# Root-mean-square norm moved behind the up projections of two feed-forward blocks

## The reference, cut to what matters

```
# first block (D_FF = 2816)
xn = rms_norm(h, g_ffn) * (1.0 + sc2) + sh2        # rms_norm: h * rsqrt(mean(h*h) + EPS) * g
up = causal_dwconv(jnp.dot(xn, w_up), conv_ffn_w, conv_ffn_b)      # 3 taps over positions
val, gte = jnp.split(up, 2, axis=-1)
h = h + ga2 * jnp.dot(jax.nn.silu(gte) * val, w_down)
# second block
u2 = rmsnorm(h, ffn_norm_w)
a, val = jnp.split(u2 @ w_up, 2, axis=-1)
a = causal_dwconv_2(a, ffn_conv_w, ffn_conv_b)
h = h + (jax.nn.silu(a) * val) @ w_down
```

## Time and profile before

| | |
|---|---|
| median of 3 runs | 1895.46 us (1890.78 to 1900.73) |
| profiled execution, its own time | 1897.88 us |
| its span, first to last instruction | 1896.1 us |
| TensorE (PE) busy | 1804.7 us, 95% |
| GpSimd (POOL) busy | 1412.7 us, 75% |
| VectorE (DVE) busy | 942.8 us, 50% |
| ScalarE (ACT) busy | 641.6 us, 34% |
| mean granted TensorE clock | 0.974 of 2.4 GHz |

### The profile page before, as it was taken

The page is one execution under the profiler, slowest core; times in us unless marked ns, Lnnn a source line. Parts: engine busy times, 40 slices in busy tenths (PEclk is TensorE's granted clock), DMA queues, the critical chain, the costliest instruction groups (busy, mean ns, idle before and its releaser), DMA issues.

```text
span 1896.1 us, 31183 instructions
## 1 busy us (share of the span) xinstructions
PE 1804.7 (95%) x10268; PEld 1541.9 (81%) x10268; DVE 942.8 (50%) x1508; ACT 641.6 (34%) x870; POOL 1412.7 (75%) x2245
## 2 busy tenths in 40 slices
PE   4999998999889999999899999999999899999997
PEld 2767775578678888887899999999999889999885
DVE  6538887745554444311655654665654333333101
ACT  3236662310144444201533443344342233333100
POOL 2768982469968888899666775776776588888885
PEclk8999997999999999999999999999999899999999
DMA  8332332334422323233122222222222222323332
GB/s 319 110 107 94 95 106 100 100 133 155 155 74 92 94 94 100 90 109 100 56 68 78 78 67 67 68 78 68 75 71 68 67 89 88 100 88 94 103 102 88
DMA packets 54298, 184.40 MB, mean 97 GB/s; under 512 B 6673, under 2 KB 7857, under 8 KB 54226
## 3 DMA queue, kind: packets, MB, share of 16 engines
q1 hardware_dynamic: 48690, 169.20, 28.0%
q10 hardware_dynamic: 5536, 14.16, 2.1%
HBM read 178.62 MB, written 4.72 MB: 97 GB/s over the span
## 4 chain that ended last, share of the span: by engine, by line
PE 67%; POOL 14%; issue 10%; DMA 3%; DVEq 2%; DVE 2%; ACT 1%; SPq 1%; POOLq 0%; ACTq 0%
PE gp L373 21%; PE gp L374 21%; PE gp L375 20%; POOL Wlo L364 9%; POOL Whi L361 3%; PE A L673 3%; DMA raw<-units 2%; POOL probe L360 2%; DVEq L1415 2%; DMA AW<-ada 1%; PE A L702 0%; PE A L721 0%; SPq L309 0%; DVE XX L1413 0%; PE A L723 0%
## 5 line engine op out<-in xcount | busy, mean ns | idle before, releaser
L364 POOL TENSOR_TENSOR Wlo<-raw,Whi 128x256 fp32r<-128x256 f32 x1120 | 932.9, 854 | 46.7
L373 PE MATMUL gp<-XNhi,Whi 128*128 128x264 f32 (+3 forms) x2384 | 790.6, 332 | 44.9 <-DVE XNlo L1063 33.2
L374 PE MATMUL gp<-XNlo,Whi 128*128 128x264 f32 (+3 forms) x2384 | 781.0, 328 | 0.0
L375 PE MATMUL gp<-XNhi,Wlo 128*128 128x264 f32 (+3 forms) x2384 | 777.5, 326 | 0.0
L373 PEld LDWEIGHTS gp<-XNhi,Whi 128*128 128x128 f32 x2384 | 455.0, 191 | 96.1 <-issue 30.1
L374 PEld LDWEIGHTS gp<-XNlo,Whi 128*128 128x128 f32 x2384 | 455.2, 191 | 40.0 <-issue 1.9
L375 PEld LDWEIGHTS gp<-XNhi,Wlo 128*128 128x128 f32 x2384 | 454.4, 191 | 38.4
L360 POOL TENSOR_TENSOR probe<-raw 1x1 f32<-1x1 f32 x560 | 156.2, 279 | 415.5 <-PE gp L375 374.1
L361 POOL TENSOR_SCALAR Whi<-raw 128x512 fp32r<-128x512 f32 x560 | 347.0, 620 | 0.0
L374 PE MATMUL gp<-AClo,Whi 128*128 128x512 f32 x352 | 139.9, 397 | 0.0
L373 PE MATMUL gp<-AChi,Whi 128*128 128x512 f32 x352 | 139.9, 397 | 0.0
(11 more groups left out here) (291 smaller groups left out, 2261.4 us busy)
## 6 DMA issues: line engine op xcount, KB each, us to landing
raw<-units SPq DMA_DIRECT2D x280, 512.0 KB, 3.5
AW<-ada SPq DMA_DIRECT2D x16, 512.0 KB, 8.8
AWL<-ada SPq DMA_DIRECT2D x16, 512.0 KB, 4.0
AWL<-ada ACTq DMA_DIRECT2D x16, 512.0 KB, 4.3
bias_rows<-RB ACTq DMA_DIRECT2D x1, 2560.0 KB, 15.0
H<-xT SPq DMA_DIRECT2D x1, 2048.0 KB, 8.7
BIAS<-bias_rows ACTq DMA_DIRECT2D x1, 2048.0 KB, 9.6
out<-H SPq DMA_DIRECT2D x8, 256.0 KB, 2.1
```

The lines of the kernel that those rows point to most:

```text
L364: ins = pool.tensor_tensor(lo[:, c:c + UNIT // 4], src[:, c:c + UNIT // 4], hi[:, c:c + UNIT // 4].bitcast(F32), ALU.subtract)
L373: pe.matmul(dst, Whi[s][:, k, :], rhi, start=start, stop=False)
L374: pe.matmul(dst, Whi[s][:, k, :], rlo, start=False, stop=False)
L375: return pe.matmul(dst, Wlo[s][:, k, :], rhi, start=False, stop=stop)
```

## The change

For norms 1 and 3 (`WEIGHTED`), those of the two up projections, `norm_split` and `norm_apply` go. As soon as a chunk of H is final, during OUT1 and OUT2, ScalarE makes XNhi = H * factor behind the square, and VectorE XNlo = H * factor - XNhi behind the residual. TensorE does the statistics in the middle of the first pair of UP instead of ahead of it. For norms 2 and 4 nothing moves.

The outputs are multiplied by RSTD on VectorE on their way from PSUM to a buffer ZZ in SBUF, and all convolution taps then read ZZ instead of PSUM. In UP1 both units of a pair are 514 columns wide instead of 512: the two columns ahead of the first position (meta positions 14 and 15) hold the shift vector, so that the output there is W(s). BC = W(s) * (sum of the three taps, TAPS) + bias is the activation's bias, and ZZ's two first columns are -W(s), which cancels it where the convolution looks ahead of the first position. The meta columns of XN, written early before, are written after UP1. A PSUM buffer is freed by the product with RSTD. ScalarE's Silu table is loaded ahead of both loops. Semaphores, the two buffers' declarations and unchanged neighbours are left out here:

```diff
--- before.py
+++ after.py
+        TAPS = sb("TAPS", [P, FC, 2])
+        BC = sb("BC", [P, 2])
...
+            ZZ = sb("ZZ", [P, 2, 2 + S], frame=f)
...
+        WEIGHTED = (1, 3)
...
                 return mm
 
-            def first_pair(u0, g0, f, halves):
+            def first_pair(u0, g0, f, halves, midway=None):
 
                 lag = 1
                 for j in range(KC + lag):
+                    if j == KC // 2 and midway is not None:
+                        midway()
                     for c, k in ((0, j), (1, j - lag)):
                         if 0 <= k < KC:
...
-            def with_stats(m, product, begin):
+            def all_units(product, begin):
 
                 begin(product)
                 with pe.Fori(1, KC // 2) as i:
                     product(i, 0)
                     product(i, 1)
-                stats(m)
...
-            def up(u0, g0, f, halves):
-
-                first_pair(u0, g0, f, halves)
+            def up(u0, g0, f, halves, m):
+
+                first_pair(u0, g0, f, halves, lambda: stats(m))
                 with pe.Fori(1, FC) as i:
                     for c, (n, c0) in enumerate(halves):
                         pe.wait_ge(gp_free[c], slot_free(g0) + i)
                         unit(u0 + i * 2 + c, c, gp[c], n, XNhi, XNlo, c0, range(KC), last=KC - 1).then_inc(unit_done, 1)
 
-            with_stats(1, *plain(U_OUT, G_OUT, MGhi, MGlo, 0, S, (merge_done, 1)))
-            up(U_UP, G_UP, 1, ((S, META), (S, META)))
-            with_stats(2, *down(U_DN, G_DN, (act_done, 1)))
+            all_units(*plain(U_OUT, G_OUT, MGhi, MGlo, 0, S, (merge_done, 1)))
+            up(U_UP, G_UP, 1, ((S + 2, META - 2), (S + 2, META - 2)), 1)
+            all_units(*down(U_DN, G_DN, (act_done, 1)))
+            stats(2)
...
-            with_stats(3, *plain(U_OUT2, G_OUT2, M2hi, M2lo, META - 2, S + 2, (mix2_done, 1)))
-            up(U_UP2, G_UP2, 3, ((S + 2, META - 2), (S, META)))
-            with_stats(4, *down(U_DN2, G_DN2, (act2_done, 1)))
+            all_units(*plain(U_OUT2, G_OUT2, M2hi, M2lo, META - 2, S + 2, (mix2_done, 1)))
+            up(U_UP2, G_UP2, 3, ((S + 2, META - 2), (S, META)), 3)
+            all_units(*down(U_DN2, G_DN2, (act2_done, 1)))
+            stats(4)
...
                     h = H[:, k, q["c0"]:q["c0"] + q["n"]]
                     act.activation(sq[:, k % 2, 0:q["n"]], h, ACT.Square).then_inc(sq_ready, 1)
+                    if m in WEIGHTED:
+                        act.activation(XNhi[:, k, q["c0"]:q["c0"] + q["n"]], h, ACT.Identity,
+                                       scale=scale_bias(m, k)[0]).then_inc(xhi_ready, 1)
...
-                    act.wait_ge(nt_ready, KC * f + k + 1)
+                    act.wait_ge(nt_ready, KC * (f // 2) + k + 1)
                     act.activation(XNhi[:, k, o0:o0 + n], nt[:, k % 3, 0:n], ACT.Identity,
...
             norm_stats(1, lambda k: load_late(3 * KC + 2 + k) if k < KC - 2 else None)
-            norm_apply(1)
-
+
+            act.preload_act_table(ACT.Silu)
             with act.Fori(0, FC) as i:
-                def fv(c):
-                    return V[:, bass.ds(VEC["ffn"] + i * 8 + c, 1)]
-                act.wait_ge(unit_done, U_UP + i * 2 + 1 + 2)
-                act.wait_ge(act_done, i + 1)
-                act.activation(YV[:, :], gp[0][:, 0:S], ACT.Identity, bias=fv(3), scale=fv(2)).then_inc(yv_first, 1)
-                act.wait_ge(unit_done, U_UP + i * 2 + 2 + 2)
-                act.activation(YG[:, :], gp[1][:, 0:S], ACT.Identity, bias=fv(7), scale=fv(6)).then_inc(yg_first, 1)
+                for c, (y, first) in enumerate(((YV, yv_first), (YG, yg_first))):
+                    act.wait_ge(z_ready, i * 2 + c + 1)
+                    if c == 0:
+                        act.wait_ge(act_done, i + 1)
+                    act.activation(y[:, :], ZZ[:, c, 2:2 + S], ACT.Identity, bias=BC[:, c:c + 1],
+                                   scale=V[:, bass.ds(VEC["ffn"] + i * 8 + (4 * c + 2), 1)]).then_inc(first, 1)
                 act.wait_ge(yg_ready, i + 1)
                 act.activation(SL[:, :], YG[:, :], ACT.Silu).then_inc(silu_ready, 1)
             norm_stats(2)
@@ -1026,15 +1036,14 @@
                     act.activation(HRS[:, :], HRS[:, :], ACT.Exp, scale=-0.5).then_inc(orstd_ready, 1)
 
             norm_stats(3)
-            norm_apply(3)
-
+
+            act.preload_act_table(ACT.Silu)
             with act.Fori(0, FC) as i:
                 def fw(c):
                     return V[:, bass.ds(VEC["ffn2"] + i * 4 + c, 1)]
-                b0 = region(S + 2)
-                act.wait_ge(unit_done, U_UP2 + i * 2 + 1 + 2)
+                act.wait_ge(z2_ready, i + 1)
                 act.wait_ge(act2_done, i + 1)
-                act.activation(YV[:, :], gp[0][:, b0 + 2:b0 + 2 + S], ACT.Identity, bias=fw(3), scale=fw(2)).then_inc(ya_first, 1)
+                act.activation(YV[:, :], ZZ[:, 0, 2:2 + S], ACT.Identity, bias=fw(3), scale=fw(2)).then_inc(ya_first, 1)
                 act.wait_ge(ya_ready, i + 1)
                 act.activation(SL[:, :], YV[:, :], ACT.Silu).then_inc(silu2_ready, 1)
             norm_stats(4)
...
                         dve.scalar_tensor_tensor(hk, src, MOD[:, bass.ds(gate + i * 2 + c, 1)], hk, ALU.mult,
                                                  ALU.add).then_inc(h_ready, 1)
                     dve.drain().then_inc(gp_free[c], 1)
+                    if m in WEIGHTED:
+                        k = i * 2 + c
+                        dve.wait_ge(xhi_ready, KC * NORMS[m]["feeds"] + k + 1)
+                        dve.scalar_tensor_tensor(XNlo[:, k, c0:c0 + n], H[:, k, c0:c0 + n], scale_bias(m, k)[0],
+                                                 XNhi[:, k, c0:c0 + n].bitcast(F32), ALU.mult, ALU.subtract).then_inc(xn_ready, 1)
...
-                for i in (range(1, KC // 2) if m == 1 else ()):
+                for i in (range(1, KC // 2) if m in WEIGHTED else ()):
                     for c in range(2):
                         add(i, c)
                         last_modulations(i, c)
                         chunk(i, c)
-                if m == 1:
+                if m in WEIGHTED:
                     return
...
-            dve.tensor_copy(XNhi[:, :, 0:META], MSQ[:, :, :])
-            dve.drain()
-            dve.tensor_tensor(XNlo[:, :, 0:META], MSQ[:, :, :], XNhi[:, :, 0:META].bitcast(F32), ALU.subtract).then_inc(meta_xn, 1)
...
             dve.scalar_tensor_tensor(AB2[:, :], MOD[:, 4 * KC:5 * KC], 1.0, vec("g_ffn", 0, KC), ALU.add, ALU.mult)
             dve.drain()
+            shift = MOD[:, 3 * KC:4 * KC].rearrange("p (k o) -> p k o", o=1)
+            for c in (META - 2, META - 1):
+                dve.tensor_copy(XNhi[:, :, c:c + 1], shift)
+                dve.drain()
+                dve.tensor_tensor(XNlo[:, :, c:c + 1], shift, XNhi[:, :, c:c + 1].bitcast(F32), ALU.subtract)
+            w = vec("ffn", 0, 8 * FC).rearrange("p (i c t) -> p i c t", c=2, t=4)
+            taps = TAPS[:, :, :].rearrange("p i (c o) -> p i c o", o=1)
+            dve.tensor_tensor(taps, w[:, :, :, 0:1], w[:, :, :, 1:2], ALU.add)
+            dve.drain()
+            dve.tensor_tensor(taps, taps, w[:, :, :, 2:3], ALU.add)
+            dve.drain()
             residual(1, U_OUT, 1, 2 * KC)
-            norm_split(1)
             dve.tensor_tensor(MOD[:, 5 * KC:], MOD[:, 5 * KC:], vec("b_ada", 5 * KC, KC), ALU.add)
...
             dve.drain()
+            dve.wait_ge(rstd_ready, 2)
             with dve.Fori(0, FC) as i:
                 def fv(c):
                     return V[:, bass.ds(VEC["ffn"] + i * 8 + c, 1)]
+                taps = TAPS[:, bass.ds(i, 1), :].rearrange("p a c -> p (a c)")
                 for c, (y, first) in enumerate(((YV, yv_first), (YG, yg_first))):
+                    b0 = region(S + 2)
+                    dve.wait_ge(unit_done, U_UP + i * 2 + c + 1 + 2)
+                    dve.scalar_tensor_tensor(BC[:, c:c + 1], gp[c][:, b0 + 1:b0 + 2], taps[:, c:c + 1], fv(4 * c + 3), ALU.mult, ALU.add)
+                    dve.tensor_scalar(ZZ[:, c, 0:2], gp[c][:, b0:b0 + 2], -1.0, None, ALU.mult)
+                    dve.tensor_tensor(ZZ[:, c, 2:2 + S], gp[c][:, b0 + 2:b0 + 2 + S], RSTD[:, 0:S], ALU.mult).then_inc(gp_free[c], 1)
+                    dve.drain().then_inc(z_ready, 1)
                     dve.wait_ge(first, i + 1)
-                    dve.scalar_tensor_tensor(y[:, 1:S], gp[c][:, 0:S - 1], fv(4 * c + 1), y[:, 1:S], ALU.mult, ALU.add)
-                    dve.drain()
-                    dve.scalar_tensor_tensor(y[:, 2:S], gp[c][:, 0:S - 2], fv(4 * c), y[:, 2:S], ALU.mult,
-                                             ALU.add).then_inc(gp_free[c], 1)
+                    dve.scalar_tensor_tensor(y[:, :], ZZ[:, c, 1:1 + S], fv(4 * c + 1), y[:, :], ALU.mult, ALU.add)
+                    dve.drain()
+                    dve.scalar_tensor_tensor(y[:, :], ZZ[:, c, 0:S], fv(4 * c), y[:, :], ALU.mult, ALU.add)
```

(25 more changed lines are left out.)

## The result

The changed kernel takes 1908.43 us (median of 9 runs, 1904.74 to 1914.88) against 1898.65 (9 runs, 1890.78 to 1903.89) for the kernel before on the same chips: a ratio of 1.0061, 95% interval 1.0041 to 1.0082. (The ratios here are taken over all the runs; they are not the quotients of the medians.) It is slower, by 9.8 us. The forecast was no measurable change, a sum of 1893.8 us, and a range of 1875 to 1907 us.

What follows compares the result with a forecast made beforehand. TensorE was taken to bound most stages, GpSimd close behind and the bound in UP1's loop after the change. From 1897.9 us, -15.4 - 4.8 + 15.1 + 1.0 = -4.1 gave 1893.8; range 1875 to 1907.

Steps and rivals of the forecast that it cites:

- VectorE's serial chain in UP1: UP1's loop: VectorE's dependent steps take 11.4 us an iteration, just below GpSimd's 11.84, so not the bound.
- its sign in the trace: UP1's loop: an iteration above 12.1 us with GpSimd idle while VectorE isn't would mean the serial chain; no chance given.
- ScalarE's instruction, twice: UP1's loop, in VectorE's chain: 0.63 us for each of two projections, taken from the Silu of that size.
- four taps, stretched: UP1's loop, in VectorE's chain: four taps of 0.75 us plus 4 x 0.26 for stretching.
- last tap to AClo's end: UP1's loop: the tail of VectorE's chain, 3.5 us, read from the trace before.
- The second switch: OUT2 to UP2: shrinks to 13.3 us from 28.7 including slow clock, a gain of 15.4 us.
- UP2's loop: Second block's up projection: GpSimd's 11.17 us just fits TensorE's 11.21 an iteration; 1.0 us lost over the loop.
- The first switch: OUT1 to UP1: TensorE waits for weights to 523.2, loop's point at 536.6 against 541.4, a gain of 4.8 us.
- The six small instructions: VectorE in OUT1, for shift columns and tap sums: delay GpSimd by 0.8 us together.
- rival C: UP1's loop: the table load stays in VectorE's chain, 12.7 us an iteration, 1909 us; chance 0.17 together with B.
- D: Rival at the switches: root late or norm rows not ready, so they don't shrink, 1908 us; chance 0.05.
- GpSimd's price of a tap: UP1's loop: each tap with two SBUF inputs costs GpSimd 0.43 us, giving 11.84 us an iteration.

Runs made afterwards that it cites:

- e3: Changed kernel, ZZ still in SBUF, with UP1's next product with RSTD put ahead of AF and YV released by AF: 1889.81 us, ratio 0.9951 to the kernel before.
- e8: e7 with the tap sums moved from OUT1 to the kernel's start: 1881.06 us, ratio 0.9921 to the kernel before.
- e2: Changed kernel with ZZ in free PSUM columns instead of SBUF, in UP1 and UP2: 1890.43 us, ratio 0.9954 to the kernel before.
- e7: e4 with the first pair of UP1 and UP2 not interleaved (first unit, statistics, second unit): 1880.72 us, ratio 0.9918 to the kernel before.
- e4: Changed kernel with both the ZZ in PSUM of e2 and the turned order of e3: 1884.59 us, ratio 0.9929 to the kernel before.
- e6: Changed kernel with VectorE's loop of UP1 written out 22 times instead of a hardware loop: 1899.01 us, ratio 1.0007 to the kernel before.

## Why the prediction was wrong, step by step

**The step that failed** is the length of VectorE's serial chain in UP1, forecast at 11.4 us, "just below GpSimd's 11.84, so not the bound". It is 12.99 in the iteration shown and 12.66 on average, and it, not GpSimd, is what the loop waits for: e3 shortened the loop by breaking the chain while every tap stayed in SBUF. The mechanism was named, and so was its sign in the trace ("if then GpSimd idles while VectorE doesn't, the serial chain"), but as a reading of the outcome and not as a rival with a price and a chance. Its terms for the iteration shown:

| term | predicted | measured |
|---|---|---|
| ScalarE's instruction, twice | 2 x 0.63 | 2 x 0.82 |
| VectorE to ScalarE, twice | 2 x 0.08 | 0.26 + 0.18 |
| four taps, stretched | 4.04 | 4.09 |
| last tap to AClo's end | 3.5 | 3.91 (AF 1.12 to 1.19, not 0.69) |
| turn of the loop | none | 0.61 |

These are 0.38, 0.28, 0.05, 0.41 and 0.61, together 1.73; small overlaps (the next BC starts 0.07 before the tap ends) and roundings (twice 3.41 had been put at 6.9) take 0.1 off, and 11.4 becomes 13.0. The first of them stood in the trace of before, where ScalarE's Identity with scale and bias on 128x512 took 780 ns:

```profile
L942 ACT ACTIVATE ffn_val<-gp,V 128x512 f32<-128x512 f32 x21 | 16.4, 780 | 0.3
```

The Silu's 0.63 was taken in its place. The turn of the loop wasn't counted at all. AF had been put down at 0.69 because it was that long in the trace of before, although had GpSimd slowed beneath it; that it would be stretched itself could not be read there.

**What held.** The second switch, 13.3 forecast and 13.0 measured. UP2's loop, 11.2. The first switch, in kind and in size: a wait on Wlo to 524.3 (523.2 forecast), the loop at 538.1 (536.6), and 1.6 us of the difference was there before OUT1 began. One term in it was mis-sized. The six small instructions ahead of the residual were priced by what they cost GpSimd, 0.8 us; they held up VectorE's first release of a gp buffer, for which TensorE waited 2.08 us. Most of that was probably covered by the wait for Wlo behind it: e8, which took two of the six away, gained nothing. ScalarE has no table load between 536 and 800 us any more, so the prediction's rival C is out, and D with it, since neither switch waits for the root. GpSimd's price of a tap held, 0.37 for 0.43, but only e3 could show it, since a longer chain covered it.

The Trainium skill (SBUF — State Buffer, "SBUF: two separate sides") has whichever of the two starts first hold the shared port pair "for the whole instruction", while the other is blocked. e3 agrees in kind and shows less in size: a tap whose length is 0.75 us alone costs GpSimd 0.37 on average, and is itself stretched to between 0.75 and 1.27; with ZZ in PSUM (e2) neither is slowed, as the section implies.

**What could not be assigned.** The -3.4 us between DN1 and OUT2's end: 1.9 lie in the mix stage, whose length varies between profiles as shown, and 1.5 in OUT2, which took 49.5 us in the kernel before and 48.0 in the changed one. It took 49.5 in e3 and e7 too, and 48.0 in e4 and e8, so the change does not decide it.

## What to carry to other kernels

When a change puts a step between two engines that used to read the same buffer independently, write out the whole cycle of dependences, every hand-over and the loop's turn included, from rows of the same operation, and treat a cycle within a microsecond of the bound as the bound. Break such a cycle first by order (the next item's first step ahead of this item's tail), then shorten it. Price an added instruction on its own engine too, and look for whoever waits behind it. And split a change by its places before you judge it: here half of it was worth 16 us and the other half cost 27.

## What the runs showed of the hardware

- A turn of VectorE's hardware loop, from AClo's end to the next iteration's first instruction, costs 0.61 us when nothing else is waited for; written out it is 0.10 (e6).
- A round trip VectorE, ScalarE, VectorE costs 0.18 to 0.26 us there and 0.14 back around a 0.82 us instruction; ScalarE's Identity took 817 ns from SBUF (changed kernel) and 780 from PSUM (the kernel before, and e2).
- Contention moves when it isn't removed: taking 1.1 us of turn, gaps and waits out of an iteration lengthened VectorE's instructions by 0.8 (e6). With ZZ in SBUF and the chain as the bound, iterations alternate between 13.0 and 12.25; they are a constant 11.59 when GpSimd sets the pace (e3) and a constant 11.31 when TensorE does (e4).
- TensorE's mean granted clock over the same 4313 matmuls of the mix stage was 1.00 in one profile (changed kernel, 525.6 us busy) and 0.98 in another (e7, 533.8 us).
